# Second block's attention: head projection between its groups, softmax scaling on ScalarE, router one-hot from place and expert

## What is computed

```python
def second_block(x, ...):
    proj = h @ w_in[l] + b_in[l]
    hg_q, hg_f, hg_i, hg_g, mb_q, mb_k, mb_v, gate_a, gate_b = jnp.split(proj, split_at, axis=-1)
    y_a = hgrn2_mixer(hg_q, hg_f, hg_i, hg_g, lower_bounds[l], hg_norm_g[l]) @ w_proj_a[l]
    y_b = moba_mixer(mb_q, mb_k, mb_v, rel_bias) @ w_proj_b[l]
    mixed = (jax.nn.sigmoid(gate_a) * y_a + jax.nn.sigmoid(gate_b) * y_b) @ w_out[l]
    x = layer_norm(DN_ALPHA * h + mixed, ln1_g[l], ln1_b[l])
    ffn = hier_moe(x, w_group[l], b_group[l], w_expert[l], b_expert[l], w_gate_up[l], w_down[l])
    x = layer_norm(DN_ALPHA * x + ffn, ln2_g[l], ln2_b[l])

def hier_moe(x, ...):          # 4 groups of 8 experts, the two best of the best group
    order = jnp.argsort(expert)
    counts = jax.ops.segment_sum(jnp.ones((n_asg,), jnp.int32), expert, num_segments=N_EXPERTS)
    padded = (counts + MOE_BLOCK - 1) // MOE_BLOCK * MOE_BLOCK
    dest = pad_start[e_s] + jnp.arange(n_asg) - starts[e_s]
    ...
```

## Time and profile before

| | |
|---|---|
| median of 3 runs | 1805.36 us (1804.65 to 1805.83) |
| the profiled execution: its own time | 1806.25 us |
| its span, first to last instruction | 1804.4 us |
| TensorE busy | 1752.5 us, 97% |
| VectorE busy | 1077.5 us, 60% |
| ScalarE busy | 705.9 us, 39% |
| mean granted TensorE clock | 0.989 |
| moved by DMA | 409.71 MB, 227 GB/s over the span |

### The profile page before, as it was taken

The page is one execution under the profiler, slowest core; times in us unless marked ns, Lnnn a source line. Parts: engine busy times, 40 slices in busy tenths (PEclk is TensorE's granted clock), DMA queues, the critical chain, the costliest instruction groups (busy, mean ns, idle before and its releaser), DMA issues.

```text
span 1804.4 us, 31906 instructions
## 1 busy us (share of the span) xinstructions
PE 1752.5 (97%) x12556; PEld 1418.9 (79%) x12556; DVE 1077.5 (60%) x1919; ACT 705.9 (39%) x1119; POOL 21.2 (1%) x26
## 2 busy tenths in 40 slices
PE   9999999999999999999999999998999999999996
PEld 8999989799999999998899998997953333333332
DVE  6775565787665877669787756868772222222223
ACT  5434453463444534455644446855321101110110
POOL 0000000000000000000000001000020000000000
PEclk9999999999999999999999999998999999999998
DMA  6445333444553355531245545442769999999996
GB/s 235 181 168 199 128 136 146 63 149 173 177 201 135 140 186 195 196 141 53 94 181 180 208 176 187 141 164 94 326 251 397 429 427 428 427 427 429 427 428 259
DMA packets 42339, 409.71 MB, mean 227 GB/s; under 512 B 5304, under 2 KB 5304, under 8 KB 7056
## 3 DMA queue, kind: packets, MB, share of 16 engines
q1 hardware_dynamic: 40032, 402.21, 57.1%
q0 software_dynamic: 1936, 5.79, 1.6%
q10 hardware_dynamic: 288, 0.52, 0.1%
HBM read 405.87 MB, written 2.63 MB: 226 GB/s over the span
## 4 chain that ended last, share of the span: by engine, by line
PE 84%; DVE 10%; DMA 4%; ACT 1%; issue 1%; DVEq 0%; SPq 0%; ACTq 0%
PE ps L598 82%; DMA soon<-w_gate_up 4%; PE ps L602 2%; DVE w_lo L1655 1%; DVE h L1761 1%; DVE x_lo L1717 1%; DVE h L1765 1%; DVE rs L1697 1%; DVE arena L2028 1%; DVE arena L2056 0%; DVE small L2034 0%; DVE small L2033 0%; DVE arena L2185 0%; DMA raw<-w_units 0%; DVE zg L1725 0%
## 5 line engine op out<-in xcount | busy, mean ns | idle before, releaser
L598 PE MATMUL ps<-x_hi,w_hi 128*128 128x256 f32 (+1 forms) x2144 | 617.0, 288 | 13.1 <-DVE x_lo L1715 5.0
L598 PE MATMUL ps<-x_lo,w_hi 128*128 128x256 f32 (+1 forms) x2144 | 610.8, 285 | 0.0
L598 PE MATMUL ps<-x_hi,w_lo 128*128 128x256 f32 (+1 forms) x2144 | 609.2, 284 | 0.0
L1655 DVE TENSOR_TENSOR w_lo<-raw,w_hi 128x1024 fp32r<-128x1024 f32 (+1 forms) x352 | 441.1, 1292 | 76.8 <-ACT w_hi L1257 76.6
L598 PEld LDWEIGHTS ps<-x_hi,w_hi 128*128 128x128 f32 x2144 | 403.9, 188 | 24.8 <-issue 9.2
L1257 ACT ACTIVATE w_hi<-raw 128x1024 fp32r<-128x1024 f32 (+1 forms) x352 | 379.7, 1112 | 107.9 <-PE ps L598 83.2
L598 PEld LDWEIGHTS ps<-x_hi,w_lo 128*128 128x128 f32 x2144 | 405.9, 189 | 0.0
L598 PEld LDWEIGHTS ps<-x_lo,w_hi 128*128 128x128 f32 x2144 | 404.9, 189 | 0.2
L598 PE MATMUL ps<-hid_hi,w_hi 128*128 128x272 f32 (+1 forms) x720 | 206.0, 286 | 0.7 <-DVE hid_lo L1717 0.3
L598 PE MATMUL ps<-hid_hi,w_lo 128*128 128x272 f32 (+1 forms) x720 | 204.6, 284 | 0.0
L598 PE MATMUL ps<-hid_lo,w_hi 128*128 128x272 f32 (+1 forms) x720 | 204.0, 283 | 0.0
(11 more groups left out here) (329 smaller groups left out, 1973.2 us busy)
## 6 DMA issues: line engine op xcount, KB each, us to landing
raw<-w_units SPq DMA_DIRECT2D x144, 1024.0 KB, 4.8
soon<-w_gate_up SPq DMA_DIRECT2D x34, 2048.0 KB, 18.2
late<-w_gate_up SPq DMA_DIRECT2D x30, 2048.0 KB, 18.3
raw<-w_out_units SPq DMA_DIRECT2D x32, 1408.0 KB, 6.0
soon<-w_down SPq DMA_DIRECT2D x16, 2048.0 KB, 18.6
late<-w_down SPq DMA_DIRECT2D x16, 2048.0 KB, 18.4
bias_rows<-kT POOLq DMA_DIRECT2D x1, 1536.0 KB, 33.4
cst<-table SPq DMA_DIRECT2D x1, 1448.0 KB, 11.9
```

The source lines that it names most:

```text
L598: return nc.tensor.matmul(out_ap, lhsT, rhs, start=start, stop=stop, skip_group_check=True)
L1655: v.tensor_tensor(part(w_lo, c, 0, n), raw_slot(u, j * n, n), part(w_hi, c, 0, n).bitcast(F32), ALU.subtract).then_inc(lo_made, 1)
```

## The change

It has six parts.

1. TensorE's attention issues `scores(2)` and `scores(3)` ahead of the first turns, and the projection `pa` is cut in 4 halves of 2 tiles (`heads_out(g)`), each issued behind `outputs(g)`.
2. The scaling of the exponents moves from VectorE to ScalarE (`scale(g)`), which waits for the inverse (`inverse_made`).
3. The rounded parts `x_hi` of the operands of `pa`, `pb` and `wo` are made by ScalarE (`high`); VectorE makes the rests alone (`low`). The operands of `wo` follow as each tile of `zg` is added.
4. VectorE's order in the attention is new: `maxima(0)` before the third and fourth `finish_head`, the products with the gates for `pa` between the groups. The inverse root of the head norms' mean is taken by ScalarE straight from PSUM. ScalarE splits the second `mv` unit ahead of the exponents.
5. The statistics of three quarters of the second half of the token rows are taken before the last tile of `wo`.
6. The router's first one-hot is made from the place and the expert alone ("first"), a place of 64 or more being pushed out of range; `cnt`, the further blocks and the full destination come behind it.

```diff
@@ attention, TensorE
+                for g in range(2, ahead):
+                    scores(g)
                 for g in range(groups):
-                    if g + 2 < groups:
+                    if g + 2 < groups and g + 2 >= ahead:
                         scores(g + 2)
                     turns_of(g)
                     if g:
                         outputs(g - 1)
+                        if between is not None:
+                            between(g - 1)
                 outputs(groups - 1)
+            def heads_out(g):
+                u0, T = plan["pa"]
+                u, half = u0 + g // 2, g % 2
+                c = arrive(u, half)
+                for j in range(2):
+                    t = T.at(2 * g + j)
+                    bank = free(t)
+                    for k in range(4):
+                        if g == j == 0:
+                            pe.wait_ge(x_ready, 80 + k + 1)
...
-                   MOBA_SEGS, MOBA_TURNS, moba_ready, values)
-            for name, at in (("pa", 0), ("pb", 4)):
...
+                   MOBA_SEGS, MOBA_TURNS, moba_ready, values, 4, heads_out)
@@ attention, ScalarE
                 def outputs(g):
                     t = V.at(g)
+                    if operands is not None:
+                        operands(g, filled(t)[:, 0:SEQ])
...
+                def scale(g):
+                    at = 16 + (g % 3) * 16
+                    act.wait_ge(inverse_made, g + 1)
+                    for u in range(4):
...
+                        nc.scalar.activation(p, p, ACT.Copy, scale=small[:, at + 12 + u:at + 13 + u]).then_inc(p_ready, 1)
+            def heads_parts(g):
+                if g == -1:
+                    split_to(plan["pa"][0])
+                elif g:
+                    split_to(*((plan["pa"][0] + 1, 1), (plan["pa"][0] + 1,), (plan["pb"][0], 1))[g - 1])
+                else:
...
+                        high(i, b_a[:, i * SEQ:(i + 1) * SEQ], SEQ)
@@ attention, VectorE
+                    if not sinks:
+                        v.reciprocal(small[:, at + 12:at + 16], small[:, at + 8:at + 12]).then_inc(inverse_made, 1)
+                        return
...
+            def early(g):
+                if g == 0:
+                    split_to(plan["pa"][0], 1)
+                    dve.wait_ge(head_made, 4)
+                    for i in range(4):
+                        low(i, SEQ, src=b_a[:, i * SEQ:(i + 1) * SEQ])
+                elif g < 3:
+                    gated_heads(2 * g - 2)
+                    gated_heads(2 * g - 1)
...
-                did(v.tensor_tensor(tile(zg, i, SEQ), tile(zg, i, SEQ), gate, ALU.add))
-            own()
-            for i in range(KT):
-                to_x(i, tile(zg, i, SEQ), SEQ)
+                v.tensor_tensor(tile(zg, i, SEQ), tile(zg, i, SEQ), gate, ALU.add).then_inc(scaled, 1)
+                if 1 <= i <= 4:
+                    last_operand(i - 1)
@@ statistics
+                if i == 7:
+                    dve.wait_ge(late_turned, 2)
+                    for p in range(2):
+                        v.bn_stats(stats_of(p, 1), ps[plan["xtok"].at(2 * p + 1)[0]][:, 0:384])
@@ router, VectorE
+            then(v.tensor_scalar(r_["over"], bank[:, 0:64], float(SLOTS), None, ALU.is_ge))
+            v.scalar_tensor_tensor(r_["em"], r_["over"], FAR, bank[:, 64:128], ALU.mult, ALU.add).then_inc(evac[t[0]], 1)
             mine(t)
...
+            destinations("first")
...
-            choose().then_inc(parts_made, 1)
+            choose("first").then_inc(parts_made, 1)
             dve.wait_ge(parts_made, 1)
-            choose_2().then_inc(p_made, 1)
+            choose_2("first").then_inc(p_made, 1)
+            rows_low(0, 1)
+            rows_low(1, 0)
+            rows_low(1, 1)
...
+            then(v.tensor_tensor(r_["em"], r_["em"], r_["over"], ALU.add))
+            destinations("dest")
```

More of the change, by code:

```diff
@@ L884, in _, with attend @@
             rotate(3)
-            def attend(names, groups, first, pbs, pTs, second, row, q_of, k_of, v_of, segs, turns, done, values=None):
+            def attend(names, groups, first, pbs, pTs, second, row, q_of, k_of, v_of, segs, turns, done, values=None,
+                       ahead=2, between=None):
                 S, TT, V = (plan[x] for x in names)
@@ L1456, in _, with attend @@
             split_to(plan["sq"][0] + 4)
-            def attend(names, groups, first, pbs, pTs, second, row, turns, o, sinks, between=None):
+            def attend(names, groups, first, pbs, pTs, second, row, turns, o, sinks, between=None, operands=None):
                 S, TT, V = (plan[x] for x in names)
@@ L1483, in attend @@
                         exponents(g + 1)
-                    if g == 0 and between is not None:
-                        between(1)
                     if g >= 2:
@@ L1493, in attend @@
                         base += cols
+                    if not sinks:
+                        if g + 1 < groups:
+                            scale(g + 1)
+                        between(g)
                     if g:
@@ L2015, in _, with attend @@
             rotate(7)
-            def attend(names, groups, first, pbs, second, row, masks_of, sinks, between=None, values=None):
+            def attend(names, groups, first, pbs, second, row, masks_of, sinks, between=None, values=None, early=None,
+                       turns_each=0):
                 S = plan[names[0]]
```

265 lines of the change are left out of this document (160 added, 105 removed).

## The result

The changed kernel takes 1811.84 us in the median (9 runs, 1810.45 to 1819.15), and the kernel before 1805.83 in the runs beside it (9 runs, 1804.20 to 1811.21). The ratio of the two is 1.0043, with a 95% interval of 1.0031 to 1.0055. It is slower by about 6 us or 0.4%, where 5.4 us faster was forecast. All executions named in this document are fast ones but one of the kernel before, beside experiments 4 to 6 (2442.66 us, at a granted clock of 0.649), which the ratios and the ranges leave out.

What follows compares the result with a forecast made beforehand. TensorE, busy 97% of the span, was taken to bound the kernel, with VectorE setting the attention's pace. A gain of 7.8 less 1.5 and 0.9 gave 5.4 us: 1800.0 forecast, range 1797.0 to 1803.4.

Steps and rivals of the forecast that it cites:

- Attention, VectorE: In the attention, VectorE works 22.5 us without waiting or scalings, so TensorE turns group 2 at 1253.3, 5.3 us earlier.
- Attention, ScalarE: From group 2's turns ScalarE, with four scalings at 1.4 us, sets the pace; `pb` ends at 1280.5 against 1288.1.
- Into `wo`, gain 7.8: At `wo`'s start, first four operands are made during `pb`; second unit starts at 1288.5 instead of 1296.3, 7.8 us gained.
- Weights of `wo`, 1.5 lost: At `wo`'s fourth unit: lands at 1301.7, split at 1304.0, needed at 1302.5; a new 1.5 us wait.
- Router, 0.9 lost: Before the experts, VectorE's work ahead of L2433 grows from 17.8 to 19.7 us; 0.9 lost, between 0 and 1.9.
- To the end, one to one: From expert 0 on, any shift of L2433 passes to the kernel's end one to one.
- the clock staying down: From 1255.7 to 1280.1 TensorE stays at 1.2 GHz, turning the 5.4 gain into 5.6 lost: 1811.0; chance 0.08.
- the last rival: In the attention TensorE is granted 2.4 GHz, saving at most 2.3 us more: 1797.7; chance 0.05.
- The signs that the prediction named for being wrong: Granted clock 0.50 beyond 1256, `wo`'s fourth unit's wait over 3 or missing, or expert 0's first piece ending the chain.

Runs made afterwards that it cites:

- experiments 4 to 6: Changed kernel with: first product ahead of one-hot, 1818.64 and 1823.83 us; scaling back on VectorE, 1802.65; early statistics undone, 1802.41; GpSimd at second Silu except in 1823.83.
- experiment 1: Changed kernel with GpSimd waiting for the experts' second Silu instead of the first before its four operations on `h`: 1801.82 us, ratio 0.9979.
- experiment 4: Changed kernel with VectorE making L2560 ahead of the next one-hot: 1818.64 us with GpSimd at the second Silu, 1823.83 at the first.
- the router alone: Kernel before with only the new router (part 6), GpSimd at the first Silu: 1814.92 us; with GpSimd at the second Silu: 1809.46 us.
- experiment 2: Kernel before with GpSimd no longer waiting for the first Silu, so its four operations start some 9 us earlier: 1815.4 us, ratio 1.0052.
- the attention alone: Changed kernel with the router of before (part 6 undone, parts 1 to 5 kept), GpSimd at the first Silu: 1800.52 us, ratio 0.9971.
- the first of experiment 7: Changed kernel with VectorE making the next one-hot, weights and moved destinations behind the block's last rows, GpSimd at the first Silu: 1801.59 us, ratio 0.9968.

## Why the prediction was wrong

Right or wrong, step by step, in the terms of the prediction:

- **Attention, VectorE.** Turns of group 2 at 1253.3: measured 23.55 from S, which is 1252.65 on the clock of before. Right to 0.7. The 1.97 us wait ahead of the second `mv` unit is gone.
- **Attention, ScalarE.** Four scalings 1.4: they took 1.48 to 1.50, and the next operation began 1.4 behind them. Output of group 1 at 1255.7: 1255.1 (1262.03 less 6.9); of group 2 at 1261.3: 1261.1; of group 3 at 1265.0: 1264.9. The rule of the Trainium skill ("ScalarE: Activation LUTs", section "Rules for kernel authors") that would send the scaling to VectorE was right in direction, and the difference is small in float32: VectorE's four take 0.92 before the next row begins, ScalarE's 1.4, and the whole shows no difference.
- **Into `wo`, gain 7.8.** `pb` ends at 1280.3 on the clock of before, forecast 1280.5. The first product of `wo` stands at 1282.4 (1289.30 less 6.9), forecast 1281.25: 1.2 late, since VectorE splits `wo`'s unit (two halves, 2.3 us) ahead of `pb`'s fifth and sixth tiles. The first unit of `wo` needs both of their banks, and TensorE waits 2.12 us, until the sixth is read. The second unit begins 0.8 later than forecast: 7.0 won. A term that was slightly too large.
- **Weights of `wo`, 1.5 lost.** The fourth unit is split from 1308.67 on, 1301.8 on the clock of before; forecast 1301.7. The landing was right. TensorE's wait was 0.49 instead of 1.5, because it came 1.2 late itself. At the last turn the gain is 5.5 in this pair of traces and 6 to 7 in most, where the two terms gave 6.3.
- **Router, 0.9 lost.** This is the step that failed: "all that stood before L2433 still does, and more ... 17.8 + 1.9 is 19.7". From the first low row to the first product there passed 28.16 us (1326.57 to 1354.73), not 19.7. The one-hot's rows take 9.74 of it instead of 1.50: 8.24 us. I had priced VectorE's rows by their durations in the trace before, as if nothing could run beside them. GpSimd doesn't appear in the prediction, though its four rows stood in the trace of before, 0.1 us behind the row that I named as critical, and the kernel's text releases them by the very Silu that I forecast to come 2 us earlier. VectorE's own work was priced well: with GpSimd later (experiment 1) the same way takes 19.93 (1320.19 to 1340.12). What I counted as nothing, the statistics, gave 0.75 back there between the last turn and the first low row (7.09 instead of 7.85), so that the product came 27.49 behind the last turn, 0.3 later than before instead of 0.9.
- **To the end, one to one.** Right: from the second block's product to the end pass 446.26 to 446.69 us in both kernels and in ten of the twelve experiments. The two others are those of experiment 4. But a wait of TensorE costs more than itself: the block behind it took 2.66 us more after the 11.08 us, and 1.60 more after 2.83. The length of the wait does not order these costs: with the router alone the block took 1.48 more after 11.08 us and 2.70 more after 2.83.

The sum with the measured terms: 5.4 won as forecast, 8.2 lost to GpSimd, 2.7 to the clock behind it: 5.5 slower. From S to the end the trace has 581.1 against 575.3, 5.8 slower; the medians have 6.0. Experiment 1, which takes the collision alone away, measured 1801.82, where the prediction stood at 1800.0. In the traces its gain from S to the end is 3.8 (575.3 to 571.5): 5.4 at the product, as forecast, less the 1.60 of low clock behind the remaining wait, which the prediction hadn't either. The medians of that pair are 4.8 apart. That the 5.4 comes out to the tenth is partly luck. At the fourth unit of `wo` 6.2 were won (forecast 6.3), but 0.7 more was lost up to the last turn in the changed kernel's trace, 0.52 of it in the wait for L2371, and the router cost 0.3 instead of 0.9; and in the traces with the attention of before the last turn varies by 1.7.

None of the rivals was this. The one that forecast a slower kernel was the clock staying down, and there the clock rose (0.90, and 1.00 in 1268.00 to 1287.00). That was the premise of the last rival, but its 2.3 us did not show: ScalarE's chain set the outputs' times, and they came as forecast. The signs that the prediction named for being wrong looked at the clock and the fourth unit's wait, which both came out well, and none looked at GpSimd. The rule was at hand: the Trainium skill ("SBUF — State Buffer", section "SBUF: two separate sides") says that VectorE and GpSimd share one pair of ports, and that whichever starts first holds it for its whole instruction against an operation with two SBUF inputs, or one in a mode that reads through both ports. By that rule each of VectorE's four one-hot operations waits out one of GpSimd's, 4 times 2.4 us; the trace agrees, with 9.7 us, and the reductions of experiment 2, which have one input, weren't held.

That the new order in the attention is good is shown by the attention alone (ratio 0.9971), and that the new router costs with the release at the first Silu is shown by the router alone (1.0055). With the later release its cost is seen in traces only. Why the clock in the first block is lower in some executions than in others (0.76 and 0.90 in the same stretch), and why the block behind a wait takes 1.5 us more in one trace and 2.7 in another, stays open; no run here was made for it.

## What to carry to other kernels

Before an engine's work is brought forward, list what its signal releases on the other engines, GpSimd above all, and look at which rows those will then lie beside; a wait such as "after the first Silu" may be a place and not a dependency. Price a row by its duration in the trace only for as long as its neighbours stay where they are. And an edit in a loop is priced by all of its rounds and up to the next thing that the other engine waits for: what brought one product 2.4 us forward won 0.2 us in its own round, and cost 2.5 in each of seven others.

## What the runs showed of the hardware

- While GpSimd ran a two-operand float32 operation on 128x1024 (2.34 to 2.55 us), VectorE's TENSOR_SCALAR, TENSOR_TENSOR and SCALAR_TENSOR_TENSOR rows with all tensors in SBUF lasted until GpSimd's operation ended, whatever their size: 1.82 us on 1x8 elements, 2.4 on 128x256 (0.31 alone). In the one-hot there was one such row to each of GpSimd's operations; two TENSOR_TENSOR rows on 128x128 passed together behind one (1.82 us for both in experiment 1, 0.48 alone). TENSOR_REDUCE and RECIPROCAL beside them weren't held up (0.41 and 0.17 us), nor were rows that read PSUM (L2437 of the kernel before, a TENSOR_SCALAR, 0.41 at 1345.08).
- GpSimd was held up where it came second. Its operations took 2.34 to 2.55 us but for one: the first of experiment 2, begun 0.02 us behind one of VectorE's TENSOR_SCALAR rows in SBUF, took 2.98, and that row and the two behind it weren't held up (0.41, 0.41 and 0.13 us).
- A wait of TensorE of 2.83 us was followed by a block at a granted clock of 0.88 that took 1.60 us longer; without the wait the same block took 12.85 us at 1.00. In seven traces with a wait of 2.83 to 3.03 or of 11.08 us in front, the block took 14.31 to 15.56 us, at 0.89 to 0.82, in no order with the wait.
- Executions of one kernel differ by 8 us and more (1810.45 to 1819.15). Two of the long ones were profiled (the changed kernel and the first of experiment 7), and both have S at 1236.00 and 1236.55 and a clock of 0.76 in 825.00 to 860.00, a stretch that is the same in all kernels; the twelve other traces have S at 1227.79 to 1231.11 and 0.85 or 0.90 there.
